# First norm of a hybrid decoder layer: the weight vector loaded as one row and copied over the partitions by PE, and all of x turned before the forget chunk

## What is computed

```python
h_res = jnp.concatenate([meta, x], axis=1)
...
hn = rms_norm(h_res, norm_mix_gain[l])      # x * rsqrt(mean(x*x) + eps) * g
w_l = w_in[l]
part = lambda i: hn @ w_l[:, o[i]:o[i + 1]]
q = part(0).reshape(B, T, N_HEADS, HEAD_DIM)
...
fg = part(3) + b_forget[l]                  # 16 columns
glu_in = part(4) + b_glu[l]
gate_attn = jax.nn.sigmoid(part(5))
gate_conv = jax.nn.sigmoid(part(6))
```

## Time and profile before

| | us |
|---|---|
| median of 3 runs | 977.45 (976.29 to 978.54) |
| the profiled execution, its own time | 977.84 |
| span of the profiled execution | 976.0 |
| PE busy | 955.8 |
| DVE busy | 601.6 |
| ACT busy | 406.3 |
| first matmul of the GLU loop | 26.57 |

### The profile page before, as it was taken

How to read it: one execution, slowest core, us unless ns; L and a number is a source line. 1 busy time by engine, 2 the same in 40 slices (tenths; PEclk the granted TensorE clock), 3 DMA queues, 4 the chain that set the end, 5 groups by cost and what they waited for, 6 DMA issues and landing times.

```text
span 976.0 us, 14595 instructions
## 1 busy us (share of the span) xinstructions
PE 955.8 (98%) x5342; PEld 820.6 (84%) x5342; DVE 601.6 (62%) x920; ACT 406.3 (42%) x701; POOL 30.2 (3%) x45
## 2 busy tenths in 40 slices
PE   5999999999999999999999999999999999999997
PEld 4999998888888888887788888788888888888886
DVE  6566678788787887875775665543344334434433
ACT  6422345455454554544683244432143224223322
POOL 2000010000000000001200000000000000000000
PEclk9999999999999999999999999999999999999999
DMA  8333332121212121222232532233333223332322
GB/s 224 88 87 96 96 86 68 47 66 44 65 43 65 45 63 44 65 66 65 70 103 87 191 90 87 86 106 91 106 87 108 87 86 107 90 104 87 90 82 87
DMA packets 153433, 84.27 MB, mean 86 GB/s; under 512 B 3023, under 2 KB 151503, under 8 KB 153392
## 3 DMA queue, kind: packets, MB, share of 16 engines
q1 hardware_dynamic: 152768, 83.37, 29.5%
q0 software_dynamic: 592, 0.29, 0.2%
q10 hardware_dynamic: 32, 0.07, 0.1%
HBM read 81.55 MB, written 2.16 MB: 86 GB/s over the span
## 4 chain that ended last, share of the span: by engine, by line
PE 95%; DVE 3%; DMA 1%; ACT 1%; issue 0%; SPq 0%; DVEq 0%
PE pj L991 61%; PE pj L987 19%; PE pTO L1094 5%; PE pTO L1092 2%; PE pTO L1080 2%; PE pS L1068 1%; PE pS L1067 1%; DVE cv L854 1%; PE pj L1236 1%; DMA ga<-in_x_dram 1%; PE pTO L1078 1%; PE pj L1015 1%; DVE ga L962 1%; PE pTO L1149 0%; PE pTO L1138 0%; DVE in_lo L706 0%
## 5 line engine op out<-in xcount | busy, mean ns | idle before, releaser
L451 ACT ACTIVATE w_hi<-raw 128x1024 fp32r<-128x1024 f32 x145 | 152.4, 1051 | 161.5 <-PE pj L991 131.1
L991 PE MATMUL pj<-in_hi,w_hi 128*128 128x512 f32 x512 | 205.5, 401 | 0.5 <-DVE w_lo L687 0.5
L991 PE MATMUL pj<-in_lo,w_hi 128*128 128x512 f32 x512 | 205.6, 402 | 0.0
L687 DVE TENSOR_TENSOR w_lo<-raw,w_hi 128x1024 fp32r<-128x1024 f32 x145 | 178.6, 1231 | 42.4 <-ACT w_hi L451 42.4
L991 PE MATMUL pj<-in_hi,w_lo 128*128 128x512 f32 x512 | 201.5, 394 | 0.0
L744 DVE SCALAR_TENSOR_TENSOR cv<-u,prm,cv 128x512 f32<-128x512 f32 (+1 forms) x240 | 181.6, 759 | 9.5 <-DVE cv L744 5.8
L991 PE MATMUL pj<-mid_hi,w_hi 128*128 128x512 f32 x368 | 144.4, 392 | 0.0
L991 PE MATMUL pj<-mid_hi,w_lo 128*128 128x512 f32 x368 | 143.3, 389 | 0.0
L991 PE MATMUL pj<-mid_lo,w_hi 128*128 128x512 f32 x368 | 143.2, 389 | 0.0
L991 PEld LDWEIGHTS pj<-in_hi,w_hi 128*128 128x128 f32 x512 | 96.4, 188 | 22.7 <-DVE w_lo L687 1.0
L991 PEld LDWEIGHTS pj<-in_hi,w_lo 128*128 128x128 f32 x512 | 96.5, 188 | 18.8
(11 more groups left out here) (186 smaller groups left out, 984.3 us busy)
## 6 DMA issues: line engine op xcount, KB each, us to landing
raw<-in_w_in_dram SPq DMA_DIRECT2D x57, 512.0 KB, 3.8
raw<-in_w_mlp_up_dram SPq DMA_DIRECT2D x32, 512.0 KB, 4.0
raw<-in_w_mlp_down_dram SPq DMA_DIRECT2D x32, 512.0 KB, 3.7
raw<-in_w_attn_out_dram SPq DMA_DIRECT2D x8, 512.0 KB, 3.7
raw<-in_w_conv_out_dram SPq DMA_DIRECT2D x8, 512.0 KB, 3.7
raw<-in_w_out_dram SPq DMA_DIRECT2D x8, 512.0 KB, 3.7
ga<-in_x_dram SPq DMA_DIRECT2D x4, 512.0 KB, 7.3
cv<-in_x_dram SPq DMA_DIRECT2D x1, 2048.0 KB, 8.7
```

Of the source, the lines that this page charges most:

```text
L451: A(w_hi[:, c % SPLIT, :], raw[:, c % RAW, :], ACT.Copy).then_inc(s_hi, 1)
L687: V.tensor_tensor(w_lo[:, c % SPLIT, :], raw[:, c % RAW, :], w_hi[:, c % SPLIT, :].bitcast(F32), ALU.subtract).then_inc(s_lo, 1)
L991: last = mm(prod(c), wt, src[:, at:at + NT], **flags)
```

## The change

Three things change.

- SP loads the gain as one row of 4 KB (`gain_row`, one partition of `u`) at the same place in its list.
- PE multiplies a column of ones (from `f_one`, which DVE has set) with this row, in two float32 matmuls of 512 columns, and so writes the gain to all 128 partitions of the PSUM area `pj[:, 0, :]`. Ahead of them it waits for the ones (`s_one`) and for the row (`s_g1`). DVE waits for the new signal `s_gp`, and reads the gain from PSUM in its scalings.
- PE turns all five pieces one after the other, and does the 24 products of the forget chunk's first half behind them in one piece.

```diff
-        gain_in = u[:, D:2 * D]
+        gain_row = u[0:1, D:2 * D]
+        gain_all = pj[:, 0, :]
...
+        s_gp = sem("s_gp")
...
                 if t == 0:
-                    sp.dma_start(gain_in, norm_mix_gain[0].partition_broadcast(P)).then_inc(s_g1, 16)
+                    sp.dma_start(gain_row, norm_mix_gain).then_inc(s_g1, 16)
...
-            dve.wait_ge(s_g1, 16)
+            dve.wait_ge(s_gp, 1)
...
-                                       in1=gain_in[0:n, :], op0=ALU.mult, op1=ALU.mult).then_inc(s_xs, 1)
+                                       in1=gain_all[0:n, :], op0=ALU.mult, op1=ALU.mult).then_inc(s_xs, 1)
...
+            pe.wait_ge(s_one, 1)
+            pe.wait_ge(s_g1, 16)
+            for h in range(2):
+                last = mm(gain_all[:, h * NT:(h + 1) * NT], bc[0:1, 0, 0:P], gain_row[:, h * NT:(h + 1) * NT],
+                          start=True, stop=True)
+            last.then_inc(s_gp, 1)
             pe.wait_ge(s_const, 8)
-            for i in range(QT):
+            for i in range(QT + 1):
                 tokens_transpose(i, ORDER[i])
 
             pe.wait_ge(s_lo, 1)
             pe.wait_ge(s_inlo, 3)
-            forget_products(0, 0, KT // 2)
-            tokens_transpose(QT, ORDER[QT])
-            forget_products(0, KT // 2, KT)
+            forget_products(0, 0, KT)
```

## The result

| | before | changed |
|---|---|---|
| median, us | 977.49 (976.29 to 978.54, 6 runs) | 980.67 (980.13 to 981.37, 6 runs) |
| ratio | | 1.0034, 95% interval 1.0021 to 1.0047 |
| the profiled execution, its own time | 977.84 | 980.21 |
| its span | 976.0 | 978.4 |
| first matmul of the GLU loop | 26.57 | 29.02 |

The changed kernel is slower by 3.2 us. No run of it stands at 980.67: three lie at 980.13 to 980.22 and three at 981.12 to 981.37, and the median is the middle between the two groups. The profiled execution is of the first group. In the two profiled executions the span grew by 2.4 us and the first GLU matmul moved by 2.45: the whole loss lies ahead of the GLU loop, and what comes behind it is the old program, shifted.

A forecast was written before the change was run, and what follows sets the result against it. PE was taken to bound the kernel, busy 98% of the span, so only its entry into the GLU loop could move: 26.57 to 28.7, +2.2 us on 977.84, giving 980.0 us, range 978.0 to 981.7.

The forecast's parts named there:

- The row's landing: SP's queue at the start: the 4 KB gain row lands at 5.1 us, bounds 4.6 to 6.7.
- The copy: PE's two float32 matmuls spreading the gain take 3.6 us at 1.2 GHz, so DVE starts at 8.7, not 6.72.
- From DVE's start to the third tile: DVE's list from 8.7: x's third tile is scaled at 13.4 instead of 12.19, +1.2 us.
- From the third tile on: DVE runs without a gap, its instructions unchanged, until x's last tile is scaled at 19.5 instead of 18.28.
- The order: PE's last stretch before the GLU loop: transposes no longer held back 1.2 us, but all 24 products come after them.
- The clock: PE's last stretch: lower level from 19.6 for 3.7 us, transposes 1.7 us, nine products at 0.22, fifteen at 0.12.
- The rival of the high clock: PE's clock is already high when the last tile is turned: +0.5 us, 978.3, chance 0.12.
- the sum: First GLU matmul at 28.7 against 26.57, +2.2 us on the profiled 977.84, giving 980.0.
- same: Whole kernel: a time that can't be told from no change, about 0.2%, 975.5 to 979.4 us; chance 0.30.
- cheap copy: PE's gain copy has an early row or the full clock, DVE starts at about 7.0: +0.5 us, 978.3, chance 0.10.
- faster: Early row and full-clock copies at once, DVE starts at 6.5: -1.9 us, 975.9, chance 0.04.
- The clock stays low through the whole first half: All 24 first-half forget products on PE run at 0.22 us: +3.6 us, 981.5, chance 0.10.

The follow-up runs named there:

- the kernel with the full queue: The changed kernel plus an unused 512 KB transfer to 128 partitions right behind the gain row on SP's queue: 980.41 us against 980.67.
- filled kernel before: The kernel before plus 8 small float32 matmuls on constants in PE's pause between the third tile's transposes and the forget products: 976.29 us, 0.9984 of before.
- copy, early products: The changed kernel's gain row and PE copy, but 12 of the first half's 24 forget products again ahead of the last tile's transposes: 977.96 us, 1.0009 of before.
- copy, new order, filled pause: The changed kernel plus 14 discarded products of the forget chunk's form in PE's idle time ahead of the last tile's transposes: 978.71 us.

## Why the prediction was right, point by point

The forecast was slower, 980.0 with 978.0 to 981.7, and 980.67 was measured. The mechanism was the forecast one, a copy that costs more than the row saves and a cover that is lost; the closeness of the last stretch is luck, as told below. Against its own chain:

- **The row's landing: right.** 5.1 was said; the row had landed at 5.09 and PE began at 5.22, near the low end of the bounds. That is 3.77 us after its issue; the landing at 3.4 that the prediction also priced didn't come.
- **The copy: right, 0.15 us short.** Said 3.6 at 1.2 GHz, measured 3.75. The reading of the pace against the granted clock shown was the step that mattered: at 2.4 GHz the copy would have been 1.87 us. DVE's first reciprocal was at 9.01 (8.7 said).
- **From DVE's start to the third tile: right size, wrong words.** Said 13.4, found 13.55. The prediction credited 0.8 us to the tiles' earlier landing; the kernel with the full queue shows that this landing is worth nothing there.
- **From the third tile on: 0.2 us missed.** "From there DVE is without a gap" was the step. From this scaling to the last one it was 4.80 us before (12.19 to 16.99) and is 5.01 now (13.55 to 18.56): DVE waits at 14.97 for ACT's copy of the first tile, which waits for its transposes at the lower clock. The last tile's scaling ended at 19.84 (19.5 said).
- **The order: right, with its reason.** PE is the bound from the last tile to the end, and the early products' cover is gone. With the level at 1.00 throughout the forget products, the GLU loop begins at 25.03 (filled kernel before), 26.64 (copy, early products) and 27.46 (copy, new order, filled pause). So the copy costs 1.6 us and the order 0.8 on top of it, 2.4 in all; the times agree (976.29, 977.96, 978.71). The order alone, with the pause filled, wasn't run, so that its share without the copy isn't shown at this clock.
- **The clock: right cost, wrong place, and that is luck.** Said: PE done with the third tile's transposes by 16.6, a pause of about 3 us, the lower level from 19.6, and nine products under it. Found in the profiled execution: the third tile's transposes until 17.3 (all at the lower clock), a pause of 2.61, the last tile's transposes at the full clock, then 15 products under the lower level, until 24.3. The transposes' 0.8 us less and the six products' 0.6 more nearly cancel (19.90 to 29.02 is 9.1 us, as 19.6 to 28.7 was). Two errors of opposite sign, not a right reading of the clock, put this stretch in its place. The rival of the high clock was half true: the level was up when the last tile was turned. It fell right after, and the rival's 978.3 came only where the pause was filled (978.71).
- **The rest of the 0.67 us.** The profiled executions differ by 980.21 - 977.84 = 2.4 us, close to the 2.2 of the sum. The sum's 980.0 is thus near the lower group of the changed kernel's runs (980.2); the median is 0.5 above it because the other three runs lie at 981.1 to 981.4. Measured against their filled versions, the changed kernel lost 2.0 us to the clock (980.67 - 978.71) and the kernel before 1.5 (977.8 - 976.29). That half microsecond belongs to the clock and was not in the sum, which compared one execution of each. With the 2.4 it makes the 2.9 by which 980.67 lies above 977.8; the 3.2 of the first table is against that table's own median of 977.49.
- **The chances.** A tenth of the forecast's 0.64 is 0.06, and the sum for "same" used 0.08; nothing hangs on it.

The rivals: "cheap copy" and "faster" fell with the copy's pace. "The clock stays low through the whole first half" (first GLU matmul at 30.2, 981.5) doesn't fit the profiled execution, whose 24 products took 4.45 us and not 5.3. But it nearly fits the profiled executions of the kernel with the full queue and of the one with two more one-row matmuls (30.14 and 30.16, 981.57 and 981.43), and by their times the upper group of the changed kernel's own runs (981.12 to 981.37). Its 0.10 was too little.

## What to carry to other kernels

A load made smaller is worth the time by which it lands earlier, less what has to replace it. Here PE could begin on the row at 5.22, where DVE had begun with the broadcast gain at 6.72: 1.5 us earlier, and the replacement, an fp32 copy by PE at its lower clock, took 3.75. Of DVE's wait of 2.92 us only 1.0 could have been won in any case, because ACT's root for the meta tokens was ready at 5.7. Work that an engine does while it would otherwise wait is cover, and moving it behind the wait costs its length (0.8 us here); on PE the pause itself costs clock as well (2.0 us here, 1.5 in the kernel before). Where runs of one kernel fall into groups a microsecond or two apart, look at PE's pauses at the start, and try to fill them before anything is redesigned. Look at all runs too, and not at the median alone: here one median stood between two groups, and another hid a gain that the spans show.

## What the runs showed of the hardware

- Eight small matmuls on constants in a pause of 2.3 us made the kernel before 1.5 us faster and took its runs' spread from 2.6 to 0.4 us. The three groups of times were PE's clock.
- Matmuls with one row of weights kept PE busy for 7.3 us (1.60 to 8.9) and its level was still low at 11.85 (eight transposes in 1.97 us). With 128-row matmuls in place of the first half of them the median fell by 1.7 us (980.84 to 979.14; 1.2 by the medians of the spans, 978.5 and 977.3), though in the profiled execution the level was low at 12.32 there too. In the kernel before nothing but transposes had run on PE when its pace doubled in the group at 13.54.
- The granted clock of the profile reads 1.00 up to the first recorded change, while the pace of the instructions (0.21 us per transpose of 128 columns) is that of the lower level. At the start of a kernel the pace has to be read, not the clock.
- A transfer to 127 partitions held up x's next tile on its queue until 28.5 us and cost 18.2 us, where one to 128 partitions in the same place cost nothing (980.41 against 980.67).
- PE can write a vector to all partitions with 8 transposes of one column read 128 times over: 1.94 us at the lower clock, against 3.75 us for the product with ones.
